# Last mixer's projections: where an output is turned, who copies it, and who begins its convolution

## The chip, the cores and the metric

The kernel runs on one core of a Trainium2 chip. A core has TensorE (PE, matrix products, results in PSUM banks), VectorE (DVE), ScalarE (ACT), GpSimd (POOL) and DMA queues, here issued mostly by SyncE (SP). Each engine runs its own instructions in program order and waits on semaphores for the others. The metric is the device time of one execution in microseconds; lower is better.

## The reference, cut to what matters

The program is a small network on 256 positions of width 1024: a block with two attention mixers, then a block of FFN, hybrid mixer, FFN. The change lies in the hybrid mixer, in the part that makes its queries, keys and values:

```python
def _dwconv(x, w):
    """Centred zero-padded depthwise conv over positions. x: (B,S,C), w: (K,C), K odd."""
    k_taps = w.shape[0]
    pad = k_taps // 2
    s = x.shape[1]
    xp = jnp.pad(x, ((0, 0), (pad, pad), (0, 0)))
    y = xp[:, 0:s] * w[0]
    for i in range(1, k_taps):
        y = y + xp[:, i:i + s] * w[i]
    return y
...
    proj = u @ w_in
    ca_b, ca_c, ca_v, dn_qkv, dn_z, dn_ba, gate_logits = jnp.split(proj, SPLIT_OFFSETS, axis=-1)
    y_a = ca_b * _dwconv(ca_c * ca_v, conv_a)
    qkv = jax.nn.silu(_dwconv(dn_qkv, conv_dn))
```

Here s is 256, dn_qkv has 3072 columns and conv_dn five taps (0 to 4; tap 2 is the middle one, which looks at the position itself). All values are float32.

## The kernel before, in words

**Products.** A product with a weight is made in float32 quality from three products in a shorter form (fp32r): high part of the left side with high part of the weight, low part with high part, high part with low part. `gemm_steps` writes one product per step. The weight comes by DMA (SP) in units of 256 rows into `ring`, which has six slots; ACT casts a unit to its high part (L486), DVE or POOL subtracts to get its low part (L491), and PE uses both (L532 and L534 for the high part, L547 for the low). A full output of 512 columns has four units, and a unit 12 products of 128x512: 8 with the high part, 4 with the low one, over two halves (tt) of 128 positions. `w_parts` has four slots, so a unit can be cast only when PE is through with the high part of the unit four before it, and the ring slot is loaded again once the low part is made. In the outputs named "qkv", "ba" and "ca", other than the first, units 0 and 2 are subtracted by DVE and units 1 and 3 by POOL (`Plan.rest_of`).

**The stage.** The projections are written one after another: qkv 0 to 5 (512 columns each), ba (416 columns), ca 0 to 2 (512 each), and later z, gate and a_out. For each qkv output j:

- ACT copies its two halves from PSUM into `tok` (L1985), which has two places by j % 2.
- PE turns it (`qkv_turns`, `turn`, L609): eight 128x128 transposes into two PSUM banks, the two blocks b = 2j and 2j+1, each with 2 x 128 channels on the partitions and 256 positions along them.
- The block is copied into `padded` with two zeros at either side (L622): the even block by ACT, the odd one by DVE.
- DVE makes the convolution in `conv_acc` (`mix_conv`): tap 0 as a multiplication (L1822, two instructions of 128x256), taps 1 to 4 as multiply and add (L1824, eight instructions).
- ACT takes the silu (L1832) into `qkT` or `vT`.

The places of `padded` and `conv_acc` go by b % 2.

**What sets the order.** There is no scheduler: each engine's program is written out. `mix_pe` writes the products of output j, then the transposes of output j-1. `mix_act` writes, for each j, the two copies to `tok`, the casts up to half an output or an output ahead (`stream_ahead`, `stream_to`), then copy and silu of block 2j-2 and silu of block 2j-1. `mix_dve` writes the subtractions ahead, the odd copies and the taps block by block. After qkv come, on ACT, the sigmoids of ba (a table load first), the copies of ca and the squares of the queries and keys, and on PE a sum for each square (L2112). The casts of ca 1 and ca 2 stand behind the last silu on ACT.

Of the kernel before, what the change touches and what calls it, by code (L numbers as in the profile page):

```python
# [42 lines left out]
SUMS = 4  # L43
TURN_BEHIND = (16, 10, 4)
# [246 lines left out]
def second_turns():  # L291
    t = turns("norm2", 4, "dve") + turns("ffn1_h", FFN_OUTS, "dve") + turns("norm3", 4, "dve")
    t += turns("qkv", 12) + turns("prod", 2) + turns("cab", 2, "dve") + turns("v", 4) + turns("grow", 1, "act")
    t += turns("y_b", 4, "dve") + turns("merged", 4, "dve")
    return t + turns("norm4", 4, "dve") + turns("ffn2_h", FFN_OUTS, "dve")
# [35 lines left out]
def build(nc, A, const_ap, out, last_block=2):  # L331
    ctx = ExitStack()
    with ctx:  # L333
# [1475 lines left out]

        def mix_conv(dve, b, link):  # L1810
# [3 lines left out]
            if b >= 2:  # L1814
                dve.wait_ge(qkv_ready, b - 1)
            for tap in range(5):
                for h in range(2):
                    c = 2 * b + h
                    w = cols[:, 1, tap * (QKV // P) + c:tap * (QKV // P) + c + 1]
                    a, src = conv_acc[:, b % 2, h, :], p[:, h, tap:tap + T]  # L1820
                    if tap == 0:
                        ins = dve.tensor_scalar(a, src, w, None, ALU.mult)  # L1822
                    else:
                        ins = dve.scalar_tensor_tensor(a, src, w, a, ALU.mult, ALU.add)  # L1824
                if tap < 4:
                    link(ins)
# [7 lines left out]
        def copy_padded(who, b):  # L1834
            if turn_reader("qkv", b) == who:
                eng = ENG[who]
                await_turn(eng, "qkv", b)
                if b >= 2:
                    eng.wait_ge(conv_done, b - 1)
                copy(eng, padded_out(b), turn_bank("qkv", b).rearrange("p (h t) -> p h t", h=2)).then_inc(turn_read[who], 1)  # L1840

        def mix_dve(dve, link):
# [5 lines left out]
            for b in range(12):  # L1848
                after = ("qkv", b // 2 + 1) if b < 10 else ("ba", 0)
                stream_ahead("dve", *after)  # L1850
                copy_padded("dve", b)
                await_turn(dve, "qkv", b)
                stream_ahead("dve", *after, 2)
                mix_conv(dve, b, link)
                if b == 9:

                    for tt in range(TT):
                        await_output(dve, "ba", 0, tt)
                        dve.tensor_tensor(sp_x[:, tt, :], gemm_bank("ba", 0, tt)[:, 16:32], head_row[:, 16:32],
                                          ALU.add).then_inc(bank_free["dve", tt], 1)  # L1860
                    for tt in range(TT):
                        dve.wait_ge(bank_free["dve", tt], plan.free_count("dve", tt, plan.outputs["ba", 0][0]))

                    dve.scalar_tensor_tensor(sp_abs, sp_x, -1.0, sp_x, ALU.mult, ALU.max).then_inc(sp_ready, 1)
# [109 lines left out]
        def mix_act(act):  # L1974
# [4 lines left out]
            for b in range(12):  # L1979
                if b % 2 == 0:  # L1980
                    for tt in range(TT):
                        await_output(act, "qkv", b // 2, tt)
                        if b >= 4:
                            await_turn(act, "qkv", b - 3)
                        act.copy(tok[:, (b // 2) % 2, tt, :], gemm_bank("qkv", b // 2, tt)[:, :]).then_inc(  # L1985
                            bank_free["act", tt], 1)
                    stream_ahead("act", "qkv", b // 2, 2)
                if b >= 2:
# [720 lines left out]
```

## Time and profile before

| | |
|---|---|
| Time, median of 3 runs | 1373.81 us (1369.03 to 1379.53) |
| The profiled execution's own time | 1375.45 us |
| Its span in the trace | 1373.7 us |
| Mean granted TensorE clock | 0.925 of full speed |
| PE busy | 1204.4 us (88%) |
| DVE busy | 877.5 us (64%) |
| ACT busy | 543.4 us (40%) |
| POOL busy | 286.1 us (21%) |

The span runs from the first to the last instruction of the profiled execution. Busy shares are means over the whole program, and the stages have different limits, so they don't say what a change in one stage is worth. The qkv outputs 1 to 5, ba and ca 0 to 2 take from 716.2 to 856.1 us of the span. A granted clock of 1.00 is TensorE's level of 2.4 GHz, 0.50 its level of 1.2 GHz.

### The profile page before, as it was taken

The numbers are of one execution on the slowest core, as the hardware profiler recorded it, in microseconds if no ns is written. First come the engines' busy times: TensorE is split into PE (matmuls) and PEld (weight loads), VectorE is DVE, ScalarE is ACT, GpSimd is POOL, SyncE is SP. The second block draws the span as 40 slices with busy tenths as digits, with TensorE's granted clock in tenths as the row PEclk, the third lists the DMA queues.
The fourth block names the chain that finished last, engine by engine and source line by source line (L and its number), as shares of the span: only waits on it lengthen the run. The fifth ranks groups of instructions, "written<-read, shape, count | busy, mean of one in ns | idle before, by whom it ended". The sixth has DMA issues, their size and how long they took to land. (4 is left out here: it accounts for less than half of the span.)

```text
span 1373.7 us, 19952 instructions
## 1 busy us (share of the span) xinstructions
PE 1204.4 (88%) x7677; PEld 998.7 (73%) x7677; DVE 877.5 (64%) x1432; ACT 543.4 (40%) x962; POOL 286.1 (21%) x160
## 2 busy tenths in 40 slices
PE   4878896988896889999999878999798989999997
PEld 4665575766675667887877666889797967788886
DVE  4773697379856447865556785687556555555554
ACT  1232365242246353344453335334324243544443
POOL 0012042125421222441113323110313111000001
PEclk9989898899888799999999989789898989999999
DMA  7877155147745246976634335389000034555552
GB/s 267 282 244 230 62 184 169 62 155 262 241 138 170 92 138 219 323 225 199 192 118 152 112 123 154 120 261 338 1 4 2 4 102 143 169 184 184 184 169 76
DMA packets 143481, 221.62 MB, mean 161 GB/s; under 512 B 10823, under 2 KB 66715, under 8 KB 143259
## 3 DMA queue, kind: packets, MB, share of 16 engines
q1 hardware_dynamic: 140512, 216.37, 48.7%
q10 hardware_dynamic: 2875, 3.98, 0.8%
q8 instruction: 61, 1.00, 0.3%
q14 instruction: 33, 0.27, 0.1%
HBM read 219.27 MB, written 1.05 MB: 160 GB/s over the span
## 5 line engine op out<-in xcount | busy, mean ns | idle before, releaser
L532 PE MATMUL bank<-w_parts,lhs_hi 128*128 128x512 f32 (+2 forms) x960 | 399.3, 416 | 30.3 <-ACT w_parts L486 28.3
L486 ACT CAST w_parts<-ring 128x1024 fp32r<-128x1024 f32 (+2 forms) x288 | 288.7, 1032 | 280.3 <-PE bank L534 89.4
L534 PE MATMUL bank<-w_parts,lhs_lo 128*128 128x512 f32 (+2 forms) x960 | 391.7, 408 | 0.0
L491 DVE TENSOR_TENSOR w_parts<-ring,w_parts 128x1024 fp32r<-128x1024 f32 (+2 forms) x224 | 299.7, 1364 | 130.0 <-ACT w_parts L486 126.3
L547 PE MATMUL bank<-w_parts,lhs_hi 128*128 128x512 f32 (+2 forms) x960 | 276.2, 403 | 11.5 <-DVE w_parts L491 11.5
L532 PEld LDWEIGHTS bank<-w_parts,lhs_hi 128*128 128x128 f32 x960 | 191.3, 199 | 73.1 <-ACT w_parts L486 24.9
L491 POOL TENSOR_TENSOR w_parts<-ring,w_parts 128x1024 fp32r<-128x1024 f32 (+1 forms) x64 | 165.9, 2595 | 324.3 <-ACT w_parts L486 316.0
L547 PEld LDWEIGHTS bank<-w_parts,lhs_hi 128*128 128x128 f32 x960 | 183.5, 195 | 55.1 <-DVE w_parts L491 17.1
L534 PEld LDWEIGHTS bank<-w_parts,lhs_lo 128*128 128x128 f32 x960 | 191.0, 199 | 37.8
L662 DVE SCALAR_TENSOR_TENSOR ada_acc<-ring,c_act,ada_acc 128x512 f32<-128x512 f32 x203 | 176.6, 870 | 13.0 <-DMA ring<-in_ada_w 2.7
L609 PE MATMUL bank<-const,arena 128*128 128x128 f32 (+2 forms) x322 | 60.0, 340 | 34.9 <-DVE arena L1633 7.2
L609 PEld LDWEIGHTS bank<-const,arena 128*128 128x128 f32 (+2 forms) x322 | 48.3, 177 | 44.7 <-DVE arena L1633 7.3
L823 POOL TENSOR_TENSOR x<-x,xn 128x512 f32<-128x512 f32 x10 | 17.6, 1784 | 291.4 <-DVE xn L814 291.4
L532 PE MATMUL bank<-w_parts,up_hi 128*128 128x512 f32 x176 | 69.1, 392 | 0.0
L534 PE MATMUL bank<-w_parts,up_lo 128*128 128x512 f32 x176 | 68.8, 391 | 0.0
L1714 DVE TENSOR_TENSOR arena<-arena,bank 128x256 f32<-128x256 f32 x44 | 18.0, 418 | 71.2 <-ACT arena L1730 70.5
L1730 ACT ACTIVATE arena<-bank 128x256 f32<-128x256 f32 x44 | 16.6, 383 | 87.0 <-PE bank L547 85.5
L547 PE MATMUL bank<-w_parts,up_hi 128*128 128x512 f32 x176 | 48.9, 392 | 0.0
L1824 DVE SCALAR_TENSOR_TENSOR arena<-arena,cols 128x256 f32<-128x256 f32 x96 | 42.3, 482 | 1.7
L688 PEld LDWEIGHTS bank<-const,ada_acc 128*128 128x128 f32 x152 | 23.6, 234 | 24.4 <-DVE ada_acc L662 19.0
L688 PE MATMUL bank<-const,ada_acc 128*128 128x1 f32 x152 | 24.3, 281 | 19.1 <-DVE ada_acc L662 14.6
L1181 ACT ACTIVATE arena<-arena 128x128 f32<-128x128 f32 x48 | 19.3, 401 | 54.8 <-DVE arena L1138 53.6
(347 smaller groups left out, 1531.2 us busy)
## 6 DMA issues: line engine op xcount, KB each, us to landing
ring<-in_w_ffn_up SPq DMA_DIRECT2D x176, 256.0 KB, 3.9
ring<-in_w_ada SPq DMA_DIRECT2D x72, 512.0 KB, 4.7
ring<-in_ada_w SPq DMA_DIRECT2D x48, 512.0 KB, 4.6
ring<-in_w_ffn_down SPq DMA_DIRECT2D x44, 512.0 KB, 4.4
ring<-in_w_in SPq DMA_DIRECT2D x44, 512.0 KB, 4.0
ring<-in_dil_w_in SPq DMA_DIRECT2D x32, 512.0 KB, 4.2
ring<-in_nsa_w_in SPq DMA_DIRECT2D x20, 512.0 KB, 4.6
ring<-in_w_in SPq DMA_DIRECT2D x20, 416.0 KB, 4.2
```

Of the source, the lines that this page charges most:

```text
L486: eng.copy(hi, raw).then_inc(hi_ready, 1)
L491: eng.tensor_tensor(lo, raw, hi.bitcast(F32), ALU.subtract).then_inc(lo_ready[who], 1)
L532: pe.matmul(b, x_hi, w, start=(k0 + k == 0), stop=False)
L534: mm = pe.matmul(b, x_lo, w, start=False, stop=False)
L547: mm = pe.matmul(bank[2 * plan.pair[o] + tt][:, 0:n], x_hi, lo[:, k * n:(k + 1) * n], start=False, stop=last_k)
L609: mm = pe.transpose(bank[4 + i % 2][0:mout, col:col + kin], src, ident[0:kin, 0:kin])
L662: ins = dve.scalar_tensor_tensor(acc, w, s, acc, ALU.mult, ALU.add)
L688: mm = pe.matmul(sums[:, c:c + 1], acc[:, c * P:(c + 1) * P], ones[:, 0:1], start=True, stop=True)
L823: pool.tensor_tensor(x[:, tt, A_HALF], x[:, tt, A_HALF], y_gated[:, tt, :], ALU.add).then_inc(x_half, 1)
L1181: act.activation(pr[:, 0:P], m[:, 0:P], ACT.Exp, bias=self.bias[:, i, 0:1], scale=SCALE, accum_out=self.den[:, i, 0:1])
L1714: dve.tensor_tensor(up_h[:, j % 2, tt, :], up_a[:, j % 2, tt, :], gemm_bank(name + "_up", j, tt)[:, 256:512], ALU.mult).then_inc(bank_free ...
L1824: ins = dve.scalar_tensor_tensor(a, src, w, a, ALU.mult, ALU.add)
```

## The change

- **PE**: the transposes of output j-1 stand behind the first 12 products (the first unit) of output j, and no longer behind all 48.
- **ACT** copies both blocks of an output into `padded`, and also writes the middle tap: it reads the PSUM bank, multiplies by the weight of tap 2 and writes `conv_acc`, two instructions per block. The turned bank is released after that.
- **DVE** keeps taps 0, 1, 3 and 4, all as multiply and add onto `conv_acc`, and makes no copy here.
- **Order of the casts and subtractions**: `stream_part` goes up to a given unit of a given output. ACT casts the first unit of output j+2 before the copies of blocks 2j and 2j+1, the next two behind them, the fourth behind the silu of block 2j. All four units of output 1 are cast before output 0 is copied to `tok`. DVE subtracts unit 0 of output j+2 before the taps of block 2j and unit 2 before those of block 2j+1.
- The additions on the ba output (L1859) stand behind the taps of the last block, where they stood behind block 9.

```diff
--- before.py
+++ after.py
@@ -41,6 +41,7 @@
 SPLIT = 4
 POOL_STAGES = ("dil", "ffn1_up", "qkv", "ba", "ca")
 SUMS = 4
+TURN_IN_UNIT = 12
 TURN_BEHIND = (16, 10, 4)
 NORMED = (("dil", 0), ("ffn1_up", 0), ("qkv", 0), ("ffn2_up", 0))
 BESIDE = (("nsa", 4), ("nsa", 5), ("dil", 6), ("dil", 7))
@@ -290,7 +291,7 @@
 
 def second_turns():
     t = turns("norm2", 4, "dve") + turns("ffn1_h", FFN_OUTS, "dve") + turns("norm3", 4, "dve")
-    t += turns("qkv", 12) + turns("prod", 2) + turns("cab", 2, "dve") + turns("v", 4) + turns("grow", 1, "act")
+    t += turns("qkv", 12, "act") + turns("prod", 2) + turns("cab", 2, "dve") + turns("v", 4) + turns("grow", 1, "act")
     t += turns("y_b", 4, "dve") + turns("merged", 4, "dve")
     return t + turns("norm4", 4, "dve") + turns("ffn2_h", FFN_OUTS, "dve")
 
@@ -1807,22 +1808,31 @@
         def padded_out(b):
             return padded[:, b % 2, :, 2:T + 2]
 
+        def tap_weight(b, tap, h):
+            at = tap * (QKV // P) + 2 * b + h
+            return cols[:, 1, at:at + 1]
+
+        def padded_act(act, b):
+
+            await_turn(act, "qkv", b)
+            if b >= 2:
+                act.wait_ge(conv_done, b - 1)
+                act.wait_ge(qkv_ready, b - 1)
+            src = turn_bank("qkv", b).rearrange("p (h t) -> p h t", h=2)
+            act.copy(padded_out(b), src)
+            for h in range(2):
+                ins = act.activation(conv_acc[:, b % 2, h, :], src[:, h, :], ACT.Copy, scale=tap_weight(b, 2, h))
+            ins.then_inc(turn_read["act"], 1)
+
         def mix_conv(dve, b, link):
 
             p = padded[:, b % 2, :, :]
             await_turns_read(dve, "qkv", [b])
-            if b >= 2:
-                dve.wait_ge(qkv_ready, b - 1)
-            for tap in range(5):
+            for i, tap in enumerate((0, 1, 3, 4)):
                 for h in range(2):
-                    c = 2 * b + h
-                    w = cols[:, 1, tap * (QKV // P) + c:tap * (QKV // P) + c + 1]
-                    a, src = conv_acc[:, b % 2, h, :], p[:, h, tap:tap + T]
-                    if tap == 0:
-                        ins = dve.tensor_scalar(a, src, w, None, ALU.mult)
-                    else:
-                        ins = dve.scalar_tensor_tensor(a, src, w, a, ALU.mult, ALU.add)
-                if tap < 4:
+                    a = conv_acc[:, b % 2, h, :]
+                    ins = dve.scalar_tensor_tensor(a, p[:, h, tap:tap + T], tap_weight(b, tap, h), a, ALU.mult, ALU.add)
+                if i < 3:
                     link(ins)
             ins.then_inc(conv_done, 1)
 
@@ -1831,13 +1841,10 @@
             dst = qkT[:, 2 * b:2 * b + 2, :] if b < 8 else vT[:, 2 * b - 16:2 * b - 14, :]
             act.activation(dst, conv_acc[:, b % 2, :, :], ACT.Silu).then_inc(qkv_ready, 1)
 
-        def copy_padded(who, b):
-            if turn_reader("qkv", b) == who:
-                eng = ENG[who]
-                await_turn(eng, "qkv", b)
-                if b >= 2:
-                    eng.wait_ge(conv_done, b - 1)
-                copy(eng, padded_out(b), turn_bank("qkv", b).rearrange("p (h t) -> p h t", h=2)).then_inc(turn_read[who], 1)
+        PROJECTIONS = [("qkv", j) for j in range(6)] + [("ba", 0), ("ca", 0)]
+
+        def stream_part(who, i, unit):
+            stream_to(who, plan.outputs[PROJECTIONS[i]][1][unit])
 
         def mix_dve(dve, link):
             dve.memset(padded, 0.0)
@@ -1845,23 +1852,21 @@
             dve.wait_ge(pads_ready, 1)
             dve.wait_ge(rate_ready, 1)
             stream_end["dve"] = plan.outputs["a_out", 1][1][-1]
-            for b in range(12):
-                after = ("qkv", b // 2 + 1) if b < 10 else ("ba", 0)
-                stream_ahead("dve", *after)
-                copy_padded("dve", b)
-                await_turn(dve, "qkv", b)
-                stream_ahead("dve", *after, 2)
-                mix_conv(dve, b, link)
-                if b == 9:
-
-                    for tt in range(TT):
-                        await_output(dve, "ba", 0, tt)
-                        dve.tensor_tensor(sp_x[:, tt, :], gemm_bank("ba", 0, tt)[:, 16:32], head_row[:, 16:32],
-                                          ALU.add).then_inc(bank_free["dve", tt], 1)
-                    for tt in range(TT):
-                        dve.wait_ge(bank_free["dve", tt], plan.free_count("dve", tt, plan.outputs["ba", 0][0]))
-
-                    dve.scalar_tensor_tensor(sp_abs, sp_x, -1.0, sp_x, ALU.mult, ALU.max).then_inc(sp_ready, 1)
+            stream_part("dve", 1, 3)
+            for j in range(6):
+                stream_part("dve", j + 2, 0)
+                mix_conv(dve, 2 * j, link)
+                stream_part("dve", j + 2, 2)
+                mix_conv(dve, 2 * j + 1, link)
+            stream_part("dve", 7, 3)
+            for tt in range(TT):
+                await_tile(dve, "ba", 0, tt)
+                dve.tensor_tensor(sp_x[:, tt, :], gemm_bank("ba", 0, tt)[:, 16:32], head_row[:, 16:32],
+                                  ALU.add).then_inc(bank_free["dve", tt], 1)
+            for tt in range(TT):
+                dve.wait_ge(bank_free["dve", tt], plan.free_count("dve", tt, plan.outputs["ba", 0][0]))
+
+            dve.scalar_tensor_tensor(sp_abs, sp_x, -1.0, sp_x, ALU.mult, ALU.max).then_inc(sp_ready, 1)
             stream_ahead("dve", "ca", 0)
             dve.wait_ge(sp_exp, 1)
             dve.tensor_scalar(sp_u, sp_e, 1.0, None, ALU.add).then_inc(sp_sum, 1)
@@ -1976,20 +1981,22 @@
             act.activation(a_rate, head_row[:, 0:16], ACT.Exp).then_inc(rate_ready, 1)
             act.wait_ge(pads_ready, 1)
             stream_end["act"] = plan.outputs["a_out", 1][1][-1]
-            for b in range(12):
-                if b % 2 == 0:
-                    for tt in range(TT):
-                        await_output(act, "qkv", b // 2, tt)
-                        if b >= 4:
-                            await_turn(act, "qkv", b - 3)
-                        act.copy(tok[:, (b // 2) % 2, tt, :], gemm_bank("qkv", b // 2, tt)[:, :]).then_inc(
-                            bank_free["act", tt], 1)
-                    stream_ahead("act", "qkv", b // 2, 2)
-                if b >= 2:
-                    copy_or_silu_act(act, b - 2)
-            stream_ahead("act", "ba", 0, 2)
-            copy_or_silu_act(act, 10)
-            copy_or_silu_act(act, 11)
+            stream_part("act", 1, 3)
+            for j in range(6):
+                for tt in range(TT):
+                    await_tile(act, "qkv", j, tt)
+                    if j >= 2:
+                        await_turn(act, "qkv", 2 * j - 3)
+                    act.copy(tok[:, j % 2, tt, :], gemm_bank("qkv", j, tt)[:, :]).then_inc(bank_free["act", tt], 1)
+                if j:
+                    qkv_silu(act, 2 * j - 1)
+                stream_part("act", j + 2, 0)
+                padded_act(act, 2 * j)
+                padded_act(act, 2 * j + 1)
+                stream_part("act", j + 2, 2)
+                qkv_silu(act, 2 * j)
+                stream_part("act", j + 2, 3)
+            qkv_silu(act, 11)
             o = plan.outputs["ba", 0][0]
             for tt in range(TT):
                 act.wait_ge(bank_free["dve", tt], plan.free_count("dve", tt, o))
@@ -2046,10 +2053,6 @@
                 stream_ahead("act", "mix_out", 0, half - 1)
                 turned_left_act(act, "merged", (2 * half, 2 * half + 1))
 
-        def copy_or_silu_act(act, b):
-            copy_padded("act", b)
-            qkv_silu(act, b)
-
         def mix_pool(pool):
 
             pool.wait_ge(qk_sum_read, 1)
@@ -2086,11 +2089,13 @@
                 for b in (2 * j, 2 * j + 1):
                     turn(pe, "qkv", b, [(tok[:, j % 2, tt, (2 * (b % 2) + h) * P:(2 * (b % 2) + h + 1) * P], P, P,
                                          h * T + tt * P) for h in range(2) for tt in range(TT)])
-            for j in range(1, 6):
-                gemm(pe, "qkv", j, from_lhs, "norm3", 512)
-                qkv_turns(j - 1)
-            gemm(pe, "ba", 0, from_lhs, "norm3", GATE_W)
-            qkv_turns(5)
+            for i in range(1, 7):
+                steps = gemm_steps(pe, *PROJECTIONS[i], from_lhs, "norm3", GATE_W if i == 6 else 512)
+                for _ in range(TURN_IN_UNIT):
+                    next(steps)
+                qkv_turns(i - 1)
+                for _ in steps:
+                    pass
             for j in range(3):
                 gemm(pe, "ca", j, from_lhs, "norm3", 512)
 
```

How ACT's order moves, for one output in the middle of the stage (output 2; L486 is a cast, L1985 the copy to `tok`, L622 the padded copy, L1832 the silu). Before:

```order
291 L1832 ACTIVATE arena<-arena 128x512 x2
292 L486 CAST w_parts<-ring 128x1024 x2
293 L1985 COPY arena<-bank 128x512 x2
294 L486 CAST w_parts<-ring 128x1024 x2
295 L622 COPY arena<-bank 128x2x256
296 L1832 ACTIVATE arena<-arena 128x512 x2
```

The change (L487 the cast, L1990 the copy to `tok`, L1822 and L1824 padded copy and middle tap, L1842 the silu):

```order
302 L1842 ACTIVATE arena<-arena 128x512
303 L487 CAST w_parts<-ring 128x1024
304 L1990 COPY arena<-bank 128x512 x2
305 L1842 ACTIVATE arena<-arena 128x512
306 L487 CAST w_parts<-ring 128x1024
307 L1822 COPY arena<-bank 128x2x256
308 L1824 ACTIVATE arena<-bank,cols 128x256 x2
309 L1822 COPY arena<-bank 128x2x256
310 L1824 ACTIVATE arena<-bank,cols 128x256 x2
311 L487 CAST w_parts<-ring 128x1024 x2
```

The two silus now stand apart, with the copies to `tok` between them; one cast, not four with the copies among them, stands between the second silu and the padded copies; a padded block takes three instructions where it took one.

DVE at the same place, from one output's last taps to the next one's (L491 the subtraction, L1822 tap 0, L1824 the other taps, L622 the padded copy). Before:

```order
621 L1824 SCALAR_TENSOR_TENSOR arena<-arena,cols 128x256 x8
622 L491 TENSOR_TENSOR w_parts<-ring,w_parts 128x1024 x2
623 L1822 TENSOR_SCALAR arena<-arena,cols 128x256 x2
624 L1824 SCALAR_TENSOR_TENSOR arena<-arena,cols 128x256 x8
625 L622 COPY arena<-bank 128x2x256
626 L1822 TENSOR_SCALAR arena<-arena,cols 128x256 x2
627 L1824 SCALAR_TENSOR_TENSOR arena<-arena,cols 128x256 x8
```

The change (L492 the subtraction, L1834 the taps):

```order
619 L1834 SCALAR_TENSOR_TENSOR arena<-arena,cols 128x256 x8
620 L492 TENSOR_TENSOR w_parts<-ring,w_parts 128x1024
621 L1834 SCALAR_TENSOR_TENSOR arena<-arena,cols 128x256 x8
622 L492 TENSOR_TENSOR w_parts<-ring,w_parts 128x1024
```

Tap 0's multiplications and the copy are gone, and one subtraction stands between every two blocks.

## Rows read from the trace of the kernel before

**Rows 1.** Groups by line, PE, 727.4 to 856.1 us: busy us, mean ns | idle before, releaser.

```profile
L532 PE MATMUL bank<-w_parts,lhs_hi 128*128 128x512 f32 (+1 forms) x128 | 56.3, 440 | 23.2 <-ACT w_parts L486 23.2
```

**Rows 2.** Busy time by stretches: PE, PEld, DVE, ACT, POOL, granted clock, DMA share, GB/s.

```profile
759.30:776.80 17.50, 15.11 (x56) 11.95 (x56) 13.79 (x24) 6.49 (x9) 5.43 (x2) 0.80 0.36 109
870.00:880.00 10.00, 10.00 (x45) 8.10 (x44) 9.35 (x25) 2.48 (x3) 6.03 (x3) 0.86 0.00 0
```

**Rows 3.** Instructions in time, PE: start us, us, [idle before, releaser].

```profile
719.01 0.40 PE L532 MATMUL bank<-w_parts,lhs_hi 128*128 128x512 f32 x1
728.24 0.48 PE L532 MATMUL bank<-w_parts,lhs_hi 128*128 128x512 f32 x1
...
739.57 1.03 PE L609 MATMUL bank<-const,arena 128*128 128x128 f32 x8
743.47 0.80 PE L532 MATMUL bank<-w_parts,lhs_hi 128*128 128x512 f32 x1 [2.87 <-ACT w_parts L486]
744.07 0.63 PE L534 MATMUL bank<-w_parts,lhs_lo 128*128 128x512 f32 x1
...
778.77 0.39 PE L534 MATMUL bank<-w_parts,lhs_lo 128*128 128x512 f32 x1
...
832.05 0.79 PE L532 MATMUL bank<-w_parts,lhs_hi 128*128 128x512 f32 x1 [5.74 <-ACT w_parts L486]
```

**Rows 4.** Instructions in time, ACT, the silus of blocks 1 and 11.

```profile
741.86 0.63 ACT L1832 ACTIVATE arena<-arena 128x512 f32<-128x512 f32 x1 [4.36 <-DVE arena L1824]
...
828.11 0.63 ACT L1832 ACTIVATE arena<-arena 128x512 f32<-128x512 f32 x1 [4.35 <-DVE arena L1824]
```

**Rows 5.** Instructions in time, DVE, from the end of block 3 to block 5.

```profile
760.93 1.23 DVE L491 TENSOR_TENSOR w_parts<-ring,w_parts 128x1024 fp32r<-128x1024 f32 x1 [1.63 <-ACT w_parts L486]
763.85 1.64 DVE L491 TENSOR_TENSOR w_parts<-ring,w_parts 128x1024 fp32r<-128x1024 f32 x1 [1.69 <-ACT w_parts L486]
765.41 2.73 DVE L1822 TENSOR_SCALAR arena<-arena,cols 128x256 f32<-128x256 f32 x2
768.18 3.63 DVE L1824 SCALAR_TENSOR_TENSOR arena<-arena,cols 128x256 f32<-128x256 f32 x8
771.73 0.68 DVE L622 COPY arena<-bank 128x512 f32<-128x512 f32 x1
772.50 0.62 DVE L1822 TENSOR_SCALAR arena<-arena,cols 128x256 f32<-128x256 f32 x2
773.15 3.63 DVE L1824 SCALAR_TENSOR_TENSOR arena<-arena,cols 128x256 f32<-128x256 f32 x8
```

**Rows 6.** The same stretch, POOL.

```profile
764.78 2.95 POOL L491 TENSOR_TENSOR w_parts<-ring,w_parts 128x1024 fp32r<-128x1024 f32 x1 [0.38 <-ACT w_parts L486]
```

**Rows 7.** One line, DVE's taps 1 to 4: duration ns min/median/max.

```profile
L1824 DVE SCALAR_TENSOR_TENSOR arena<-arena,cols x96: 476/483/490, 733.2 to 827.6; 128x256 f32<-128x256 f32 x96
```

**Rows 8.** Instructions in time, POOL and DVE, in two earlier stages.

```profile
176.31 2.87 POOL L491 TENSOR_TENSOR w_parts<-ring,w_parts 128x1024 fp32r<-128x1024 f32 x1 [3.32 <-ACT w_parts L486]
```
```profile
177.75 1.97 DVE L662 SCALAR_TENSOR_TENSOR ada_acc<-ring,c_act,ada_acc 128x512 f32<-128x512 f32 x1
...
301.14 9.87 DVE L662 SCALAR_TENSOR_TENSOR ada_acc<-ring,c_act,ada_acc 128x512 f32<-128x512 f32 x7
...
566.59 5.68 DVE L662 SCALAR_TENSOR_TENSOR ada_acc<-ring,c_act,ada_acc 128x512 f32<-128x512 f32 x7
```

**Rows 9.** Instructions in time, ACT: four with scale and bias from memory.

```profile
703.92 1.50 ACT L928 ACTIVATE left_tmp<-bank,mod_shift,mod_scale 128x128 f32<-128x128 f32 x4 [1.14 <-issue]
```

**Rows 10.** Groups by line and form, ACT, whole span: busy us, mean ns.

```profile
L1183 ACT ACTIVATE arena<-arena 128x256 f32<-128x256 f32 x48 | 23.7, 495 | 0.0
L1181 ACT ACTIVATE arena<-arena 128x128 f32<-128x128 f32 x48 | 19.3, 401 | 54.8 <-DVE arena L1138 53.6 <-PE bank L1115 0.6
```

**Rows 11.** Instructions in time, ACT: the padded copy, and a cast in the z stage.

```profile
764.60 0.59 ACT L622 COPY arena<-bank 128x512 f32<-128x512 f32 x1
...
883.03 1.05 ACT L486 CAST w_parts<-ring 128x1024 fp32r<-128x1024 f32 x1 [10.00 <-DMA ring<-in_w_in]
```

## What the change is predicted to do

> **What bounds the kernel now.** I read the busy shares of the whole, then the waits of the stage, then each engine's instructions in order of time. From 727.4 to 856.1 us PE stands still for 23.2 us, all of it before a unit's first product and all of it waiting for an ACT cast [rows 1]. ACT is not short of time: in one output's 17.5 us it is busy 6.49, DVE 13.79, POOL 5.43 [rows 2]. The casts are late because they stand in ACT's program behind two silus, which wait for DVE's taps; the row of a silu names L1824 as what ended its wait [rows 4]. So the stage goes round a loop of DVE and ACT. Read on DVE from the end of one odd block, 1.63 us before 760.93 = 759.30, to the end of the next, 773.15 + 3.63 = 776.78, it takes **17.48 us** [rows 5]: a wait of 1.63 (silu and first cast), a subtraction, a wait of 1.69, a second subtraction, tap 0, taps 1 to 4 (3.55 from start to start), a copy, tap 0 again, taps again. Over the stage the silus of blocks 1 and 11 stand at 741.86 and 828.11 [rows 4], five outputs of 17.25 us on average (one output, ba, is narrower). PE needs less: a pass of 48 products takes 739.57 - 728.24 = 11.33 us, with the transposes (up to 1.03) about 12.3 [rows 3].
>
> Two rows in the loop are longer than their work. The second subtraction takes 1.64 us where its like takes 1.23, and the first tap 0 pair 2.73 where the second takes 0.62 [rows 5]: POOL's subtraction runs from 764.78 to 767.73 [rows 6], and DVE's tap pair gets going only when it ends. The same shows with multiply-and-adds that have two inputs in SBUF, as taps have: POOL's begins at 176.31, DVE's of 177.75 takes 1.97 us, and a chain of seven takes 9.87 us with POOL beside it and 5.68 without [rows 8]. POOL cuts into a chain; each such cut costs about what a POOL subtraction lasts, (9.87 - 5.68) / 2 = 2.1 us for the two there.
>
> **The change, part by part.**
>
> *Earlier start.* The transposes of output 0 stand behind output 1's first unit, whose products end at 719.01 [rows 3], so both blocks are turned by 719.01 + 1.03 = 720.0. ACT then needs a copy, 0.59 [rows 11], less some 0.1 of overlap, and two middle taps. No row has a 128x256 ACT instruction with a scale from memory and an input in PSUM. Four of 128x128 with two such operands take 1.50, the last alone 0.46, so 0.35 each [rows 9]; 128 more columns cost 0.495 - 0.401 = 0.09 [rows 10]; that makes 0.44. From above 0.55 (0.46 + 0.09, no overlap); from below 0.35, as at half the size. I take 0.44, so a block costs ACT 0.5 + 0.88 = 1.4 us, and block 0 is ready at 721.4. DVE then has taps 3.55, subtraction 1.14 (1.23 less 0.09 overlap), taps 3.55, and two POOL subtractions of output 2 fall into it (next point), 2 x 2.3: end of block 1 at 721.4 + 12.8 = 734.2. Today it is 741.86. **Gain 7.7 us.**
>
> *The loop.* Removed from DVE: two tap 0 pairs (0.62 each) and a copy (0.68), 1.9 us of work; two subtractions stay, one between every two blocks. The wait of 1.69 between the two subtractions goes, since the casts no longer stand in a row with the `tok` copies. Moved to ACT per output: a second copy and four middle taps, 0.5 + 1.76 = 2.3 us onto 6.49 of 17.5, which it has. But the first padded copy now stands behind silu and first cast, so from the end of an odd block to the next block's first tap it is 1.63 + 1.4 = 3.0 us; DVE's unit 0 subtraction lies inside that.
>
> What POOL does to the taps decides the rest. Today the 96 taps take 476 to 490 ns, none held up [rows 7]: POOL's two subtractions fall beside waits, the subtraction and tap 0. In the new order unit 1's cast comes behind the padded copies and unit 3's behind the even silu, so both POOL subtractions fall on taps. By rows 7 alone a tap isn't held up and costs its 3.55 per eight; by rows 8 each costs DVE some 2.1 to 2.5 us. I take 2.3: L662 is the same instruction with the same kinds of operands. Loop: 3.0 + 3.55 + 1.14 + 3.55 + 2 x 2.3 = **15.9 us** against 17.48. **Gain 1.6 x 5 = 8.0 us.** With no holding up DVE would need 11.3 and PE's 12.3 would set the pace.
>
> The Trainium skill, "SBUF — State Buffer", section "Who interferes with whom", says it as a rule: a VectorE instruction with two SBUF inputs contends with a GpSimd instruction that reads SBUF, and the second to issue is blocked until the first ends. Without the rule, by rows 7 alone, an output would take 12.3 us and the time would be rival 1's; with it an output takes 15.9. By rows 8 the trace agrees with the rule.
>
> *PE.* It now has the slack of half an output between the casts and their use. Its wait shows before the transposes, which need the `tok` copies, and these stand behind the even silu. Per output it has 15.9 - 12.3 = 3.6 us to lose, in one or two pieces. After a wait of 2.87 us products run at 0.63 us each, the level of 1.2 GHz, for a while [rows 3]; that is inside the 3.6, as the loop sets the pace. After the shorter wait before 778 they run at 0.39 at once [rows 3].
>
> *Tail.* PE's wait of 5.74 before ca 1 (832.05) is 3.9 us behind the silu of block 11 [rows 3, 4]. The casts still stand behind that silu, so it stays so relative to it; but ca 0 will end later relative to the silu, the wait shrinks to about 2 us, and the low clock behind it goes: some 6 products at 0.39 for 0.63 (an estimate, half a unit), **gain 1.3 us**. The ba additions behind the last block delay only the sigmoids by 2 small instructions, and a table load lies there already: nothing, and 1 us at most.
>
> *Behind.* The z stage waits for DMA (10.00 us before 883.03, rows 11), which moved nothing from 870 to 880 [rows 2], as the ring was full. Its next loads are released by subtractions of z, which move with PE. So the gain passes through whole; if it were half absorbed there, 8 us would be left. The number of table loads doesn't change in the order, and the transposes are as many.
>
> Sum: 7.7 + 8.0 + 1.3 = 17.0. Against the profiled execution's 1375.45 that is 1358.4; it lies 1.6 above the median, so **1357 us** against 1373.81.
>
> **Rivals.**
>
> 1. *Taps are not held up, PE sets the pace.* From 727.4, seven passes of 11.33 (qkv 2 to 5, ca 0 to 2), ba (13/16 of one, 9.2) and six sets of transposes (about 5.5): 79.3 + 9.2 + 5.5 = 94 us, so 821 where it is 856.1: 35 us, **1339**. For it: rows 7. Against it: rows 8 and the tap 0 row. Part of it can come true if POOL's work falls into DVE's wait of 3.0 us: 5 x 2.3 = 11 more, 1346.
> 2. *The ACT side of the loop is longer.* Middle taps at 0.55 and a semaphore step at each hand-over (four per output, 0.2 each) add 1.2 us per output, a third POOL cut another; the loop stays near 17.3 and only the start is won: **1366**, the change then being within 1%. For it: every price in the loop is a bound from other rows.
> 3. *Slower: TensorE stays at 1.2 GHz.* The wait is cut in pieces inside each product. If each piece brings the low level back, a pass takes 2 x 12.3 = 24.6 us where the loop takes 17.25 now: 5 x 7.3 - 7.7 = 29 more, **1403**. It decides once over 5 us of each pass's 11.3 are done at the low level, since 12.3 + 5 is today's pace. Against it: today PE waits longer per output, and the granted clock of an output with a wait was 0.80 [rows 2], not 0.5.
> 4. *Absorbed behind the stage*: 8 us left, 1366.
>
> That the change doesn't do what it says is excluded by the order of its instructions, shown above.
>
> **How the numbers follow.** Forecast 0.62 (1351 to 1362, from middle taps of 0.35 to 0.55 and cuts of 2.1 to 2.5 us). Rival 1, whole or in part, 0.15; rival 2, 0.15; rival 3, 0.03; rival 4, 0.05. 8 in 10: from 1345, which takes in rival 1 in part, to 1367, which takes in rivals 2 and 4. A difference of 1% (13.7 us) is about what a measurement of this kernel can tell. Faster by more is under 1360: rival 1 and most of the forecast, 0.72. Within 1%: rest of the forecast, rivals 2 and 4: 0.25. Slower: 0.03.
>
> **What would show it.** The first taps at about 721 and the odd block 1's silu at 734; odd silus 15.9 us apart; taps with a maximum of some 2.5 us instead of 490 ns, two of them per output; the L491 groups of DVE no longer cut; PE's wait at L609 instead of L532, 2 to 4 us per output; the last silu at about 813, ca 2 ending about 839 where it is 856; the z stage and everything behind moved by the same 17. It is wrong if taps stay at 490 ns (then rival 1), if silus come more than 17 us apart with ACT the one waited for (rival 2), or if products at 0.63 us fill whole passes (rival 3).

## The result, and the profile after

| | before | changed |
|---|---|---|
| Time, median of 4 runs | 1372.46 us (1369.03 to 1379.53) | **1354.05 us** (1352.56 to 1356.42) |
| Ratio, changed to before | | **0.9861**, 95% interval 0.9817 to 0.9904 |
| Span of the profiled execution | 1373.7 us | 1350.8 us |
| Mean granted TensorE clock | 0.925 | 0.936 |

The change makes the kernel 1.4% faster, 18.4 us (by the interval between 13 and 25). Forecast were 17. The median before takes in a fourth run; 1373.81 was that of three. In the traces the stage from the end of output 1's first unit to the end of ca 2 takes 838.95 - 720.81 = 118.1 us where it took 856.09 - 719.01 = 137.1, so 18.9 less.

The profiled execution is a further 4.0 us shorter: it comes to the stage 1.8 us later and needs 5.8 us less behind it; the medians don't show the 4.0. Most of the 1.8 us is TensorE's clock and not the change. PE waits just ahead of the stage for the same subtraction, in both kernels equally long (the kernel before, then the changed one):

```profile
710.00 0.73 PE L547 MATMUL bank<-w_parts,lhs_hi 128*128 128x512 f32 x2 [1.47 <-DVE w_parts L491]
```

```profile
710.33 1.22 PE L548 MATMUL bank<-w_parts,lhs_hi 128*128 128x512 f32 x2 [1.46 <-DVE w_parts L492]
```

Behind it the products run at 0.40 us in the first and at 0.63 in the second, until about 713.8. The changed kernel is 0.3 us late before this place and 1.8 behind it. Below, one output in the middle of the stage and the ends of it.

VectorE in order of time, from the end of block 3 to the end of block 5, which answers to [rows 5] (start us, us, engine line operation, [idle before, releaser]):

```profile
752.37 1.23 DVE L492 TENSOR_TENSOR w_parts<-ring,w_parts 128x1024 fp32r<-128x1024 f32 x1 [1.64 <-ACT w_parts L487]
753.60 5.80 DVE L1834 SCALAR_TENSOR_TENSOR arena<-arena,cols 128x256 f32<-128x256 f32 x8
759.31 1.22 DVE L492 TENSOR_TENSOR w_parts<-ring,w_parts 128x1024 fp32r<-128x1024 f32 x1
760.45 5.59 DVE L1834 SCALAR_TENSOR_TENSOR arena<-arena,cols 128x256 f32<-128x256 f32 x8
767.68 1.23 DVE L492 TENSOR_TENSOR w_parts<-ring,w_parts 128x1024 fp32r<-128x1024 f32 x1 [1.64 <-ACT w_parts L487]
```

GpSimd in the same stretch ([rows 6]):

```profile
755.80 2.40 POOL L492 TENSOR_TENSOR w_parts<-ring,w_parts 128x1024 fp32r<-128x1024 f32 x1 [7.57 <-ACT w_parts L487]
761.07 2.46 POOL L492 TENSOR_TENSOR w_parts<-ring,w_parts 128x1024 fp32r<-128x1024 f32 x1 [2.87 <-ACT w_parts L487]
```

Each of POOL's two subtractions falls on a row of eight taps, and each such row takes 5.59 or 5.80 us where it took 3.63. The line's own statistics show the single taps that stood still, which [rows 7] did not have:

```profile
L1834 DVE SCALAR_TENSOR_TENSOR arena<-arena,cols x96: 471/484/2653, 722.8 to 810.4; 128x256 f32<-128x256 f32 x96
```

The longest tap lasts 2.65 us, the median one 0.484. ScalarE, the silus of blocks 1, 3, 5 and 11, and between them the cast and the first padded copy with its two middle taps ([rows 4, 11]):

```profile
735.46 0.63 ACT L1842 ACTIVATE arena<-arena 128x512 f32<-128x512 f32 x1 [3.94 <-DVE arena L1834]
...
750.77 0.63 ACT L1842 ACTIVATE arena<-arena 128x512 f32<-128x512 f32 x1 [4.12 <-DVE arena L1834]
751.31 1.03 ACT L487 CAST w_parts<-ring 128x1024 fp32r<-128x1024 f32 x1
752.25 0.58 ACT L1822 COPY arena<-bank 128x512 f32<-128x512 f32 x1
752.72 0.84 ACT L1824 ACTIVATE arena<-bank,cols 128x256 f32<-128x256 f32 x2
...
766.08 0.63 ACT L1842 ACTIVATE arena<-arena 128x512 f32<-128x512 f32 x1 [4.11 <-DVE arena L1834]
...
810.87 0.63 ACT L1842 ACTIVATE arena<-arena 128x512 f32<-128x512 f32 x1 [5.12 <-DVE arena L1834]
```

The odd silus are 15.31 us apart, from 735.46 to 810.87 five outputs of 15.08 on average; before it was 17.48 and 17.25. TensorE ([rows 3]): the transposes of outputs 0, 2, 3, then the start of ca 1, and a row of it behind:

```profile
720.81 1.04 PE L610 MATMUL bank<-const,arena 128*128 128x128 f32 x8
...
746.75 1.06 PE L610 MATMUL bank<-const,arena 128*128 128x128 f32 x8 [1.55 <-ACT arena L1990]
...
762.07 1.94 PE L610 MATMUL bank<-const,arena 128*128 128x128 f32 x8 [3.01 <-ACT arena L1990]
...
814.82 0.50 PE L533 MATMUL bank<-w_parts,lhs_hi 128*128 128x512 f32 x1 [2.11 <-ACT w_parts L487]
...
817.40 1.91 PE L548 MATMUL bank<-w_parts,lhs_hi 128*128 128x512 f32 x4
```

The waits of 690 to 833 us (us in total, times, longest) say the same:

```profile
ACT arena L1842 <- DVE arena L1834: 38.8, 11, 5.1
...
PE bank L610 <- ACT arena L1990: 9.0, 4, 3.0
...
PE bank L533 <- ACT w_parts L487: 3.1, 2, 2.1
```

In the stage PE stands still for 11.1 us (9.0 ahead of transposes and 2.1 ahead of ca 1; the rest of the last row is an earlier 1.03), where it was 23.2 [rows 1], and now mostly for the copies to `tok`, no longer for casts.

### The profile page after: what moved, and what is told of

Read it like the earlier page. It is cut to its first block and busy times, and to the rows that moved or that the text cites. A ratio compares the mean times of both kernels' runs of the same rounds, so it can differ in the third digit from the quotient of the medians.

```text
span 1350.8 us, 19941 instructions
## 1 busy us (share of the span) xinstructions
PE 1190.0 (88%) x7677; PEld 984.2 (73%) x7677; DVE 876.9 (65%) x1402; ACT 555.7 (41%) x992; POOL 283.7 (21%) x160
## 5 line engine op out<-in xcount | busy, mean ns | idle before, releaser
L487 ACT CAST w_parts<-ring 128x1024 fp32r<-128x1024 f32 (+2 forms) x288 | 290.0, 1033 | 286.0 <-PE bank L535 87.7
L492 DVE TENSOR_TENSOR w_parts<-ring,w_parts 128x1024 fp32r<-128x1024 f32 (+2 forms) x224 | 304.5, 1384 | 112.9 <-ACT w_parts L487 112.5
L492 POOL TENSOR_TENSOR w_parts<-ring,w_parts 128x1024 fp32r<-128x1024 f32 (+1 forms) x64 | 163.6, 2557 | 312.5 <-ACT w_parts L487 287.1
L533 PEld LDWEIGHTS bank<-w_parts,lhs_hi 128*128 128x128 f32 x960 | 189.4, 197 | 50.1 <-issue 8.8
L548 PEld LDWEIGHTS bank<-w_parts,lhs_hi 128*128 128x128 f32 x960 | 181.2, 192 | 55.2 <-DVE w_parts L492 18.3
L663 DVE SCALAR_TENSOR_TENSOR ada_acc<-ring,c_act,ada_acc 128x512 f32<-128x512 f32 x203 | 172.5, 850 | 13.2 <-DMA ring<-in_ada_w 2.5
L1834 DVE SCALAR_TENSOR_TENSOR arena<-arena,cols 128x256 f32<-128x256 f32 x96 | 66.4, 733 | 1.5 <-ACT arena L1824 0.2
```

The lines of the kernel that those rows point to most:

```text
L487: eng.copy(hi, raw).then_inc(hi_ready, 1)
L492: eng.tensor_tensor(lo, raw, hi.bitcast(F32), ALU.subtract).then_inc(lo_ready[who], 1)
L533: pe.matmul(b, x_hi, w, start=(k0 + k == 0), stop=False)
L548: mm = pe.matmul(bank[2 * plan.pair[o] + tt][:, 0:n], x_hi, lo[:, k * n:(k + 1) * n], start=False, stop=last_k)
L663: ins = dve.scalar_tensor_tensor(acc, w, s, acc, ALU.mult, ALU.add)
L1834: ins = dve.scalar_tensor_tensor(a, p[:, h, tap:tap + T], tap_weight(b, tap, h), a, ALU.mult, ALU.add)
```

## The experiments

Two theories were tried against each other. **A**: the stage goes at the pace of a loop of DVE and ACT, in which a POOL subtraction makes a tap stand still for nearly its whole length; the gain is an earlier start plus a shorter loop. **B**: the hold-ups lie beside waits that are there anyway, and the pace is that of the hand-overs between the engines.

| kernel | median us | ratio to before, interval | odd silus apart, us |
|---|---|---|---|
| before | 1374.87, 1374.48 | | 17.48 |
| changed | 1354.05 (before: 1372.46) | 0.9861, 0.9817 to 0.9904 | 15.31 |
| changed, subtractions on DVE | 1338.12 | 0.9740, 0.9680 to 0.9800 | 12.31 |
| before, subtractions on DVE | 1365.96 | 0.9928, 0.9900 to 0.9956 | 16.09 |
| changed, copy ahead of the silu | 1345.28 | 0.9783, 0.9752 to 0.9814 | 13.50 |
| changed, both | 1339.65 | 0.9738, 0.9699 to 0.9776 | 12.12 |
| changed, transposes late | 1364.80 | 0.9921, 0.9875 to 0.9967 | 15.35 |
| changed, five taps on DVE | 1359.21 | 0.9890, 0.9861 to 0.9919 | 16.65 |
| changed, POOL subtracts 8 columns | 1337.83 | 0.9743, 0.9719 to 0.9766 | 12.12 |
| changed, all but 16 subtractions on DVE | **1321.93** | **0.9617**, 0.9589 to 0.9645 | 12.31 |

The first "before" median belongs to the four kernels behind "changed", the second to the last four. The last column is from an odd silu in the middle of the stage to the next.

**1. Who subtracts.** In the changed kernel:

```diff
-POOL_STAGES = ("dil", "ffn1_up", "qkv", "ba", "ca")
+POOL_STAGES = ("dil", "ffn1_up")
```

> The changed kernel, with the weight subtractions of qkv, ba and ca given from POOL to DVE. Theory A: the loop from one odd silu to the next (15.3 us measured) holds 2 x 2.15 us in which a tap stands still behind a POOL subtraction; on DVE a subtraction costs 1.14 us, and that of the fourth unit falls into DVE's wait of 1.64 for silu and cast. The loop is then 2.8 + 3.55 + 2 x 1.14 + 3.55 = 12.2 us, as long as PE's own pass (12.3), so 5 x 3.0 = 15 us less: 1339. Theory B: the hold-ups are covered by other waits, and the loop's length is that of the hand-overs between ACT, PE and DVE; then DVE's added work of 2.3 us per output is added: 1354 + 11 = 1365.

Measured 1338.1 us, loop 12.31. One loop of DVE:

```profile
751.98 1.22 DVE L492 TENSOR_TENSOR w_parts<-ring,w_parts 128x1024 fp32r<-128x1024 f32 x1
753.71 1.23 DVE L492 TENSOR_TENSOR w_parts<-ring,w_parts 128x1024 fp32r<-128x1024 f32 x1 [0.51 <-ACT w_parts L487]
754.93 3.63 DVE L1834 SCALAR_TENSOR_TENSOR arena<-arena,cols 128x256 f32<-128x256 f32 x8
758.48 2.36 DVE L492 TENSOR_TENSOR w_parts<-ring,w_parts 128x1024 fp32r<-128x1024 f32 x2
760.75 3.63 DVE L1834 SCALAR_TENSOR_TENSOR arena<-arena,cols 128x256 f32<-128x256 f32 x8
764.30 1.22 DVE L492 TENSOR_TENSOR w_parts<-ring,w_parts 128x1024 fp32r<-128x1024 f32 x1
```

DVE does two subtractions more and is through sooner: eight taps take 3.63 again, and the fourth unit's subtraction (751.98) fills the wait of 1.64. In this kernel's stage PE has no wait left at all. Its groups from 714 to 838 us (busy us, mean ns | idle before):

```profile
L533 PE MATMUL bank<-w_parts,lhs_hi 128*128 128x512 f32 (+1 forms) x149 | 59.3, 398 | 0.0
```

The 0.0 stands where [rows 1] have 23.2. PE is now the faster of the two by a little: its transposes are 12.11 us apart (752.16, 764.27), the silus 12.31, which is DVE's own round (764.30 - 751.98 = 12.32). B, which had 1365, is out.

**2. The same edit without the change**, on the kernel before.

> The kernel before, with the same edit alone: the weight subtractions of qkv, ba and ca on DVE. Theory A: tap 0 of the even block no longer stands behind POOL (2.1 us), and the two added subtractions fall into DVE's waits of 1.63 and 1.69 or replace that hold-up; the loop goes from 17.48 to about 15.5 us: 5 x 2.0 = 10 us less, 1362. Theory B: 2.3 us more DVE work per output, 1372 + 11 = 1383, or nothing if DVE isn't on the path, 1372.

Measured 1366.0, 8.9 us less than before, and a loop of 16.09; A had 1362 and 15.5. The direction is A's, the size a little under: DVE now makes units 0 and 1, waits, makes units 2 and 3, and only then comes to the taps.

```profile
759.62 2.36 DVE L491 TENSOR_TENSOR w_parts<-ring,w_parts 128x1024 fp32r<-128x1024 f32 x2 [1.63 <-ACT w_parts L486]
762.54 2.36 DVE L491 TENSOR_TENSOR w_parts<-ring,w_parts 128x1024 fp32r<-128x1024 f32 x2 [0.56 <-issue]
764.82 0.61 DVE L1822 TENSOR_SCALAR arena<-arena,cols 128x256 f32<-128x256 f32 x2
```

Tap 0's pair takes 0.61 and not 2.73 [rows 5], as expected. With POOL out of the stage the change is worth 1366.0 - 1338.1 = 28 us, with POOL in it 18. The intervals leave that difference of 10 open by as much again; the loops show it. Taking POOL out shortens the loop by 17.48 - 16.09 = 1.39 us before and by 15.31 - 12.31 = 3.00 after, since the change's order puts both of POOL's subtractions on taps: 1.6 us per output, 8 in five.

**3. The even block's copy ahead of the odd silu**, POOL as in the changed kernel.

```diff
-                if j:
-                    qkv_silu(act, 2 * j - 1)
                 stream_part("act", j + 2, 0)
                 padded_act(act, 2 * j)
+                if j:
+                    qkv_silu(act, 2 * j - 1)
                 padded_act(act, 2 * j + 1)
```

> The changed kernel with one move in ACT's order: cast of unit 0 and the padded copy with middle tap of the even block stand ahead of the silu of the odd block before, not behind it. POOL keeps its subtractions. Theory A: DVE finds the even block ready when it ends the odd one and waits neither for the cast (1.64) nor for the copy; loop 1.14 + 3.55 + 1.14 + 3.55 + 2 x 2.15 = 13.7 us instead of 15.3, so 5 x 1.6 = 8 us less: 1346. Theory B (the port decides alone, the wait lies beside it): a POOL subtraction falls where DVE waited anyway and nothing is won, 1354.

Measured 1345.3, loop 13.50. DVE has no wait left; subtractions and taps follow one another:

```profile
749.30 1.22 DVE L492 TENSOR_TENSOR w_parts<-ring,w_parts 128x1024 fp32r<-128x1024 f32 x1
750.43 5.77 DVE L1834 SCALAR_TENSOR_TENSOR arena<-arena,cols 128x256 f32<-128x256 f32 x8
756.12 1.22 DVE L492 TENSOR_TENSOR w_parts<-ring,w_parts 128x1024 fp32r<-128x1024 f32 x1
757.25 5.62 DVE L1834 SCALAR_TENSOR_TENSOR arena<-arena,cols 128x256 f32<-128x256 f32 x8
```

So the two parts of the loop are separate and each can be taken away alone: DVE's wait for silu, cast and copy (2.87 us from the last tap to the next, 1.64 of them idle; the loop is 1.81 shorter) and the two hold-ups.

**4. Both edits together.**

> Both edits on the changed kernel: subtractions of qkv, ba and ca on DVE, and the even block's copy ahead of the odd silu. Theory A: DVE needs 7.1 + 4 x 1.14 = 11.7 us per output, below PE's 12.3, so PE sets the pace and its waits before the transposes go (9.0 us in the changed kernel) with the low clock behind them: 1337 to 1339, and less than 3 us better than the kernel with the subtractions alone. Theory B: 1354 or more, as there.

Measured 1339.7; its interval (0.9699 to 0.9776) and that of experiment 1 (0.9680 to 0.9800) lie over each other. PE sets the pace at 12.12 us; what DVE is spared beyond that is worth nothing.

**5. The transposes put back.**

```diff
-                for _ in range(TURN_IN_UNIT):
-                    next(steps)
-                qkv_turns(i - 1)
                 for _ in steps:
                     pass
+                qkv_turns(i - 1)
```

> The changed kernel with its transposes put back behind all 48 products of the next output; ACT's copies, middle tap and order stay. Theory A (the gain is an earlier start plus a shorter loop): block 0 is turned three units later, 8.4 us; the loop stays at 15.3 us, since PE, which now has to wait for the second unit's cast behind the padded copies, needs 12.3 + 1.0 = 13.3 us per output. 1354 + 8 = 1362. Theory B (the start is worth nothing, since PE is busy either way; all of the gain is the loop): 1354.

Measured 1364.8, 9.7 us under the kernel before where the changed one was 18.4 under, so the early transposes are worth about 9 us (the two intervals of 0.4 to 0.5% each, some 6 us, leave that open by several us). The traces are sharper. From PE's wait ahead of the stage (710.33 in the changed kernel, 712.80 here, followed in both by products at 0.63) to the silu of block 1 (735.46 and 746.25) it is 25.13 and 33.45 us, so the start is 8.3 us earlier, against 8.4 worked out. The loop is 15.35, the changed kernel's 15.31: the place of the transposes moves the start and not the pace. PE's new wait, for the second unit's cast, is small, as here at 751.25, and lies inside the loop:

```profile
747.87 0.51 PE L533 MATMUL bank<-w_parts,lhs_hi 128*128 128x512 f32 x1 [1.80 <-ACT w_parts L487]
751.25 0.51 PE L533 MATMUL bank<-w_parts,lhs_hi 128*128 128x512 f32 x1 [0.30 <-ACT w_parts L487]
```

**6. The middle tap back on DVE**; ACT still copies both blocks.

```diff
-            act.copy(padded_out(b), src)
-            for h in range(2):
-                ins = act.activation(conv_acc[:, b % 2, h, :], src[:, h, :], ACT.Copy, scale=tap_weight(b, 2, h))
+            ins = act.copy(padded_out(b), src)
...
-            for i, tap in enumerate((0, 1, 3, 4)):
+            if b >= 2:
+                dve.wait_ge(qkv_ready, b - 1)
+            for i, tap in enumerate(range(5)):
```

(with tap 0 a multiplication again).

> The changed kernel with the middle tap back on DVE: ACT only copies both blocks, DVE makes tap 0 as a multiplication and taps 1 to 4 as before. Theory A: per output the copy's 0.5 us lies beside the unit 0 subtraction, then 2 x 4.2 us of taps, 1.14 for the other subtraction and 2 x 2.15 behind POOL: 1.64 + 1.23 + 8.4 + 1.14 + 4.3 = 16.7 us against 15.3; 5 x 1.4 = 7 us more: 1361. Theory B (DVE's work isn't what the loop is made of): ACT saves 1.8 us of middle taps per output and the time stays or falls: 1350 to 1354.

Measured 1359.2 and a loop of 16.65, against 16.7 worked out:

```profile
748.89 1.23 DVE L492 TENSOR_TENSOR w_parts<-ring,w_parts 128x1024 fp32r<-128x1024 f32 x1 [1.64 <-ACT w_parts L487]
750.04 0.61 DVE L1836 TENSOR_SCALAR arena<-arena,cols 128x256 f32<-128x256 f32 x2
750.68 5.77 DVE L1838 SCALAR_TENSOR_TENSOR arena<-arena,cols 128x256 f32<-128x256 f32 x8
```

ACT had the time for the middle tap; on DVE it is on the path. By time alone the 5 us are inside the noise of two intervals; by the loops, 1.34 us each, they are shown.

**7. POOL without its work.** In every output behind qkv 0 POOL makes the low part of units 1 and 3 for 8 columns only, so this kernel leaves out the rest of those low parts:

```diff
+                        if who == "pool" and plan.outputs["qkv", 0][1][0] < u:
+                            lo, raw, hi = lo[:, 0:8], raw[:, 0:8], hi[:, 0:8]
                         eng.tensor_tensor(lo, raw, hi.bitcast(F32), ALU.subtract).then_inc(lo_ready[who], 1)
```

> The changed kernel, in which POOL subtracts only the first 8 of a unit's 1024 (or 832) columns in all stages behind the first qkv output, so that low parts of the weights are left out of the result there. POOL still waits, starts and signals at the same places. Theory A (a tap stands still for as long as POOL's subtraction lasts): 2 x 2.15 us per output go, DVE needs 1.64 + 1.14 + 7.1 + 1.14 = 11.0 us, PE's 12.3 sets the pace: 5 x 3.0 us less and two hold-ups in the ca outputs, 1337 to 1339, with no work moved to DVE. Theory B (only the hand-over to and from POOL counts): within 3 us of 1354.

Measured 1337.8, loop 12.12. POOL and the taps:

```profile
746.75 0.20 POOL L494 TENSOR_TENSOR w_parts<-ring,w_parts 128x8 fp32r<-128x8 f32 x1 [4.95 <-ACT w_parts L487]
```

```profile
L1836 DVE SCALAR_TENSOR_TENSOR arena<-arena,cols x96: 476/480/489, 726.9 to 795.4; 128x256 f32<-128x256 f32 x96
```

Semaphores, order and DVE's work are those of the changed kernel; only the length of POOL's instruction is another, and no tap lasts over 0.489 us. That shows the cause itself: it is the time in which POOL's instruction runs.

**8. Subtractions of the dilated mixer and the first FFN on DVE** too: `POOL_STAGES = ()`. The expectation calls it every subtraction; 16 of them, of four outputs of the two attention mixers that `BESIDE` names, stay on POOL.

> The changed kernel with every weight subtraction on DVE, in the dilated mixer and the first FFN too. Theory A: there as well a POOL subtraction holds up DVE for longer (2.1 to 2.5 us) than the subtraction costs on DVE (1.14); in the first FFN PE is 95% busy and nothing is won, in the dilated mixer PE waits 10.7 us for sums made by DVE, of which some 3 to 5 go: 1334 against 1338 for the kernel with qkv, ba and ca moved. Theory B (there the hold-ups lie beside waits, and DVE has less room): 1338 or up to 5 us more.

Measured 1321.9, 16 us better than experiment 1 and 3.8% under the kernel before; A had 1334, 4 us better, so the sign was right and the size three to four times too small. The trace has it in the dilated mixer: VectorE's multiply-and-adds for the modulation (L663) there, in the kernel of experiment 1, then in this one, from one output to the next:

```profile
300.69 7.70 DVE L663 SCALAR_TENSOR_TENSOR ada_acc<-ring,c_act,ada_acc 128x512 f32<-128x512 f32 x7
308.31 3.41 DVE L492 TENSOR_TENSOR w_parts<-ring,w_parts 128x1024 fp32r<-128x1024 f32 x1
...
316.90 7.69 DVE L663 SCALAR_TENSOR_TENSOR ada_acc<-ring,c_act,ada_acc 128x512 f32<-128x512 f32 x7
```

```profile
301.35 5.69 DVE L663 SCALAR_TENSOR_TENSOR ada_acc<-ring,c_act,ada_acc 128x512 f32<-128x512 f32 x7
306.95 2.35 DVE L492 TENSOR_TENSOR w_parts<-ring,w_parts 128x1024 fp32r<-128x1024 f32 x2
...
315.76 5.69 DVE L663 SCALAR_TENSOR_TENSOR ada_acc<-ring,c_act,ada_acc 128x512 f32<-128x512 f32 x7
```

16.2 us per output have become 14.4. In the first of the two DVE's rows follow one another without a gap, and PE is busy for 15.26 of the 16.20 us; in the second PE is busy for all of the 14.41. So DVE's chain, lengthened by POOL, set the pace there, and now PE does. The expectation had counted only PE's waits for the sums (10.7 us). In the two spans (1332.0 and 1321.2) the difference of 10.8 us is there by the end of the dilated mixer, and the FFN behind it gives nothing, as expected; the medians differ by 16, and the other 5 have no place that a trace shows. This is the fastest kernel of the study.

## Why the prediction was right

Forecast 1357 (1345 to 1367), measured 1354. Its mechanism held, and its terms came out so (measured by the traces):

| term | forecast | measured | from |
|---|---|---|---|
| earlier start | 7.7 | 8.2 | silu of block 1 at 735.46, less the 1.8 by which this execution is late at 720.81, against 741.86 |
| loop, five outputs | 8.0 | 10.8 | 5 x (17.25 - 15.08) |
| tail | 1.3 | 0 | last silu to the end of ca 2: 28.08 against 27.98 |
| sum | 17.0 | 19.0 | 18.9 in the stage's traces, 18.4 in the medians |

That the sum came within 2 us is in part luck: the start and the loop were put 0.5 and 2.8 us too low, the tail 1.3 too high, and the medians can tell 18.4 only to some 6 us either way. The last silu stands at 810.87 and the end of ca 2 at 838.95, where 813 and 839 were said.

- **The loop was put 0.6 us per output too long, so its gain too small.** It said 15.9 where the middle outputs take 15.31. The time from the last tap to the next block's first was put at 3.0 and is 1.64 + 1.23 = 2.87, as the copy and the two middle taps overlap their neighbours by more than assumed. A hold-up was put at 2.3 and is 5.80 - 3.63 = 2.17 and 5.59 - 3.63 = 1.96 us. That is 0.2 and 0.5 less than POOL's instruction lasts (2.40 and 2.46), since the tap that POOL finds running is finished beside its start.
- **The choice between [rows 7] and [rows 8] decided the forecast.** By the first alone (rival 1) it would have been 1339, which is indeed what the kernels without the hold-up run at (1338.1, 1337.8). The Trainium skill, "SBUF — State Buffer", section "Who interferes with whom", has the rule: a VectorE instruction with two SBUF inputs and a GpSimd instruction that reads SBUF exclude each other. By experiment 7 the trace agrees, with taps of up to 2.65 us with POOL's full instruction and of 0.489 at most without it.
- **The tail term failed.** It said that a wait of 2 us before ca 1 would not bring the low clock. The wait was 2.11 (814.82), and from the sixth product on they run at 0.63 each; the four low products at 817.40 take 1.91 where they take 1.10 at 2.4 GHz. The first unit of ca 1 takes 819.11 - 814.82 = 4.29 us, as before (836.40 - 832.05 = 4.35), so nothing was gained. The inference from one wait in the kernel before, with no fall behind it, was too weak:

```profile
778.44 0.50 PE L532 MATMUL bank<-w_parts,lhs_hi 128*128 128x512 f32 x1 [2.37 <-ACT w_parts L486]
```

- **PE's slack** was foreseen right, if a little too large (3.6 us per output): four waits ahead of the transposes of 1.55 to 3.01 us, none of which lengthens the loop. Experiment 5 shows that the place of the transposes doesn't touch the pace, and experiment 4 that the pace becomes PE's once DVE needs less than 12.1.
- **Rival 2's hand-overs** of 0.2 us each stand in no row. The silu starts 0.03 us behind the end of the last tap (745.14 + 5.60, 750.77), the first tap 0.04 behind the middle taps (752.72 + 0.84, 753.60).
- **One reading of the rows before was incomplete.** The lengthened subtraction of 763.85 stood behind an earlier one of POOL's, which [rows 6] don't have and which ends at 764.41; only tap 0 stood behind that of 764.78. The sum doesn't depend on it.

```profile
761.93 2.48 POOL L491 TENSOR_TENSOR w_parts<-ring,w_parts 128x1024 fp32r<-128x1024 f32 x1 [11.68 <-ACT w_parts L486]
```

- **The passage through the DMA-bound stage** held. The cast behind the wait for DMA, which stood at 883.03 [rows 11], comes 18.4 us sooner:

```profile
864.66 1.05 ACT L487 CAST w_parts<-ring 128x1024 fp32r<-128x1024 f32 x1 [9.96 <-DMA ring<-in_w_in]
```

## What to carry to other kernels

Before giving half of an elementwise stream with two inputs in SBUF to POOL, compare what POOL's instruction costs DVE by standing in its way with what the work costs on DVE itself: here some 2.0 to 2.2 us against 1.14 for a 128x1024 subtraction, so that "sharing" the work slowed the engine it was to relieve. A line whose instructions all last alike says only that today's order keeps them apart from POOL; look at another line of the same form before moving work onto it. And when several engines go round in a loop, write down the loop of one of them instruction by instruction: it tells both what a change is worth and which engine is next (here PE at 12.1 us, beyond which nothing was to be won).

## What the runs showed of the hardware

- A POOL instruction gets between two of DVE's in a chain that follows without a gap; it is not kept waiting to the end of the chain. It holds that chain up once per instruction, in the middle outputs for 1.96 to 2.17 us at 2.40 to 2.46 of its own.
- Tap 0's multiplication, which has one tensor as input, was held up by POOL too: 2.73 us for two where they take 0.62 without it [rows 5] and 0.61 in experiment 2. Why that instruction is held as well, no run here shows.
- TensorE's clock after a short wait isn't told by the wait alone. In the changed kernel 1.55 us (746.75) brought no fall and 2.11 us (814.82) did, beginning at the sixth product behind it; in the kernel before 2.37 us (778.44) did not. The wait ahead of the stage, 1.46 to 1.48 us in all ten traces, was followed within four products by some at 0.63 in eight of them and by none in two (the kernel before and experiment 6). That alone moves a trace by 1.3 to 1.5 us.
- An operand from memory costs ACT little: 128x256 from PSUM with a scale from memory takes 0.489 us (median of the middle taps), a silu of the same size from PSUM without such a scale 0.383 (L1730 in the kernel before; another function, so the comparison is rough), and two middle taps in a row take 0.84. The Trainium skill, "ScalarE: Activation LUTs", section "What ACT_TABLE_LOAD costs", states some 93 ns for each such operand; here it is 106 ns.
